# Stationary token tiles begin 64 bytes further in SBUF

## The reference

```python
# first block, per layer (w_in: 1024 x 10,432, cut into 12 parts)
h = rmsnorm(x, pre_norm_g[l])
(u, v, z_a, c_q, c_kv, k_rope, z_b, x_c, z_c, g_a, g_b, g_c) = split(h @ w_in[l])
y_a = gmlp_spatial(u, v, ...) * silu(z_a)
y_b = mla_attention(c_q, c_kv, k_rope, ...) * silu(z_b)
y_c = rg_lru(x_c, ...) * silu(z_c)
merged = (sigmoid(g_a) * (y_a @ w_proj_a[l]) + sigmoid(g_b) * (y_b @ w_proj_b[l])
          + sigmoid(g_c) * (y_c @ w_proj_c[l]))
x = x + rmsnorm(merged @ w_out[l], post_norm_g[l])

# second block, per layer: a pooling mixer (layer 0) or sparse attention (layer 1), then
x = x + conv_ffn(rmsnorm_2(x, norm_ffn[i]), ffn_up[i], ffn_conv[i], ffn_conv_b[i], ffn_down[i])
gate = sigmoid(rmsnorm_2(x, norm_ple[i]) @ ple_gate[i])
x = x + gate * (p[i] @ ple_proj[i])
```

## Time and profile before

| | |
|---|---|
| median of 3 runs | 1472.91 us (1466.99, 1472.91, 1478.4) |
| span of the profiled execution, first to last instruction | 1465.8 us |
| time of the profiled execution | 1465.8 us |
| TensorE busy | 1422.5 us, 97% |
| VectorE busy | 1051.1 us, 72% |
| ScalarE busy | 871.4 us, 59% |
| DMA | 240.98 MB, mean 164 GB/s |
| mean granted TensorE clock | 0.991 |

### The profile page before, as it was taken

The page is one execution under the profiler, slowest core; times in us unless marked ns, Lnnn a source line. Parts: engine busy times, 40 slices in busy tenths (PEclk is TensorE's granted clock), DMA queues, the critical chain, the costliest instruction groups (busy, mean ns, idle before and its releaser), DMA issues.

```text
span 1465.8 us, 23062 instructions
## 1 busy us (share of the span) xinstructions
PE 1422.5 (97%) x9283; PEld 1281.7 (87%) x9283; DVE 1051.1 (72%) x1601; ACT 871.4 (59%) x1522; POOL 85.3 (6%) x138
## 2 busy tenths in 40 slices
PE   8999999999999999999999989999989999999997
PEld 8988989888789989898878789998889878999886
DVE  7736669986676447699986778884776665888746
ACT  7465756564465656575545656664683553766546
POOL 9100000006000000000000000000000000000000
PEclk9999999999999999999999999999999999999999
DMA  8614476566556344665675537766545103666553
GB/s 256 189 50 151 124 228 195 180 193 190 193 145 186 80 123 144 188 189 185 188 223 199 158 116 220 214 202 191 158 145 145 45 1 104 208 191 197 185 180 115
DMA packets 189210, 240.98 MB, mean 164 GB/s; under 512 B 19086, under 2 KB 133954, under 8 KB 189104
## 3 DMA queue, kind: packets, MB, share of 16 engines
q1 hardware_dynamic: 183232, 228.66, 51.4%
q0 software_dynamic: 5776, 10.82, 2.3%
q10 hardware_dynamic: 96, 0.03, 0.0%
HBM read 238.42 MB, written 1.05 MB: 163 GB/s over the span
## 4 chain that ended last, share of the span: by engine, by line
PE 86%; ACT 5%; DVE 5%; DMA 2%; issue 1%; DVEq 0%; SPq 0%
PE bank L620 25%; PE bank L623 25%; PE bank L624 25%; PE bank L837 2%; PE bank L1222 1%; ACT w_hi L1327 1%; DVE w_lo L1883 1%; DMA raw<-in_mla_w_ukv 1%; ACT T L1824 1%; PE bank L1179 1%; PE bank L1136 1%; ACT S L1520 1%; PE bank L774 1%; PE bank L1208 1%; PE bank L900 0%
## 5 line engine op out<-in xcount | busy, mean ns | idle before, releaser
L1883 DVE TENSOR_TENSOR w_lo<-raw,w_hi 128x1024 fp32r<-128x1024 f32 (+2 forms) x452 | 518.6, 1170 | 207.9 <-ACT w_hi L1327 204.7
L1327 ACT CAST w_hi<-raw 128x1024 fp32r<-128x1024 f32 (+2 forms) x452 | 449.4, 1009 | 271.6 <-DMA raw<-in_w_in 114.3
L620 PE MATMUL bank<-h_hi,w_hi 128*128 128x256 f32 (+1 forms) x1640 | 457.4, 279 | 6.8 <-DVE h_lo L1919 3.9
L623 PE MATMUL bank<-h_lo,w_hi 128*128 128x256 f32 (+1 forms) x1640 | 454.8, 277 | 0.0
L624 PE MATMUL bank<-h_hi,w_lo 128*128 128x256 f32 (+1 forms) x1640 | 454.6, 277 | 0.0
L620 PEld LDWEIGHTS bank<-h_hi,w_hi 128*128 128x128 f32 (+1 forms) x1640 | 308.2, 188 | 10.0 <-issue 7.8
L623 PEld LDWEIGHTS bank<-h_lo,w_hi 128*128 128x128 f32 (+1 forms) x1640 | 308.2, 188 | 0.1
L624 PEld LDWEIGHTS bank<-h_hi,w_lo 128*128 128x128 f32 (+1 forms) x1640 | 308.1, 188 | 0.0
L620 PE MATMUL bank<-w_hi,h_hi 128*128 128x512 f32 (+1 forms) x464 | 178.8, 385 | 2.7 <-DVE h_lo L1919 1.7
L623 PE MATMUL bank<-w_lo,h_hi 128*128 128x512 f32 (+1 forms) x464 | 176.7, 381 | 0.0
L624 PE MATMUL bank<-w_hi,h_lo 128*128 128x512 f32 (+1 forms) x464 | 176.6, 381 | 0.0
(11 more groups left out here) (366 smaller groups left out, 2084.9 us busy)
## 6 DMA issues: line engine op xcount, KB each, us to landing
raw<-in_w_in SPq DMA_DIRECT2D x160, 512.0 KB, 3.8
raw<-in_ffn_up SPq DMA_DIRECT2D x88, 512.0 KB, 4.5
raw<-in_ffn_down SPq DMA_DIRECT2D x40, 512.0 KB, 4.4
raw<-in_w_proj_a SPq DMA_DIRECT2D x16, 512.0 KB, 3.6
raw<-in_w_proj_b SPq DMA_DIRECT2D x16, 512.0 KB, 3.5
raw<-in_w_proj_c SPq DMA_DIRECT2D x16, 512.0 KB, 3.6
raw<-in_w_out SPq DMA_DIRECT2D x16, 512.0 KB, 3.6
raw<-in_ple_gate SPq DMA_DIRECT2D x16, 512.0 KB, 4.6
```

Of the source, the lines that this page charges most:

```text
L620: first = pe.matmul(out_, lh, rh, start=start, stop=False)
L623: pe.matmul(out_, lh, rl, start=False, stop=False)
L1327: act.copy(weights(w_hi, slot, b, size), weights(raw, slot, b, size)).then_inc(sems["hi_done"], 1)
L1883: dve.tensor_tensor(weights(w_lo, slot, b, size), weights(raw, slot, b, size), weights(w_hi, slot, b, size).bitcast(F32), ALU.subtract).th ...
```

## The change

Tiles of tokens that are only ever stationary begin 64 bytes further in SBUF. For `y2`, `ya`, `yb`, `yc` and `p` this is done in the plans of `overlay`: a gap `steps(1)` of 64 bytes is put ahead of the pair, and gaps behind it are sized so that what follows keeps its place or moves as a whole. `h_hi` and `h_lo` become views of rooms that are 32 floats longer, and a second pair of views, `s_hi` and `s_lo`, begins 16 floats on. All uses in which `h` holds merged tokens, gated tokens (the input of the ple gate) or the attention's output go to `s`; the uses as the normed input `h` stay. `sg` and `rec` get other places, and the constant `causal1` is cut from 256 to 128 columns, which makes room and leaves the values in use as they were.

Begin of the operands of `three` in the built programs, in bytes modulo 128, and the count of its matmuls:

| columns | moving | stationary | count before | count after |
|---|---|---|---|---|
| 256 | 96 (tokens) | 32 (weights) | 5124 | 5124 |
| 256 | 96 (tokens) | 96 (weights) | 108 | 108 |
| 256 | 32 (weights) | 96 (tokens) | 144 | 144 |
| 512 | 96 (weights) | 96 (tokens) | 2496 | 816 |
| 512 | 96 (weights) | 32 (tokens) | 0 | 1680 |

Of the 108, 96 are those of `keys_values` and 12 belong to a product with 48 stationary columns. The order of instructions is the same on every engine before and after, and so are their waits and shapes, except that the constants' second load has 1476 columns instead of 1604.

```diff
-                  ("mask1", TOK), ("mask0", P), ("causal1", TOK), ("cmp0", 16), ...
+                  ("mask1", TOK), ("mask0", P), ("causal1", P), ("cmp0", 16), ...
-    put("causal1", np.where(k <= q + P, 0.0, -1e30))
+    put("causal1", np.where(k[:, :P] <= q, 0.0, -1e30))
...
+        def steps(n):
+            return (None, [P, SHIFT * n], F32)
...
-        h_hi = sb("h_hi", [P, KT, TOK], F32R)
-        h_lo = sb("h_lo", [P, KT, TOK], F32R)
+        h_room = [sb(name, [P, KT * TOK + 2 * SHIFT], F32R) for name in ("h_hi", "h_lo")]
+        h_hi, h_lo = (t[:, 0:KT * TOK].rearrange("p (k n) -> p k n", n=TOK) for t in h_room)
+        s_hi, s_lo = (t[:, SHIFT:SHIFT + KT * TOK].rearrange("p (k n) -> p k n", n=TOK) for t in h_room)
...
-             ("zc", [P, LT, TOK], F32)],
+             steps(2), ("zc", [P, LT, TOK], F32), ("rec", [P, 1, TOK], F32)],
...
-             ("yb_hi", [P, KT, TOK], F32R), ("yb_lo", [P, KT, TOK], F32R),
+             steps(1), ("yb_hi", [P, KT, TOK], F32R), ("yb_lo", [P, KT, TOK], F32R),
...
-             ("uz", [P, KT, TOK], F32), ("rec", [P, 1, TOK], F32), ("wsT", [P, GM_GROUPS, P], F32),
-             ("bs", [P, GM_GROUPS, P], F32), ("yc_hi", [P, LT, TOK], F32R), ("yc_lo", [P, LT, TOK], F32R)],
-            [kb(20), ("G", [P, KT, TOK], F32), ("ya_hi", [P, KT, TOK], F32R), ("ya_lo", [P, KT, TOK], F32R)],
+             ("uz", [P, KT, TOK], F32), steps(14), ("wsT", [P, GM_GROUPS, P], F32),
+             ("bs", [P, GM_GROUPS, P], F32), ("yc_hi", [P, LT, TOK], F32R), steps(2), ("yc_lo", [P, LT, TOK], F32R)],
+            [kb(20), ("G", [P, KT, TOK], F32), steps(1), ("ya_hi", [P, KT, TOK], F32R), ("ya_lo", [P, KT, TOK], F32R)],
...
-            [(None, [P, 9, TOK], F32), ("p_hi", [P, L * 2, TOK], F32R), ("p_lo", [P, L * 2, TOK], F32R), kb(3),
-             (None, [P, KT, TOK], F32),
-             ("y2_hi", [P, FT, TOK], F32R), ("y2_lo", [P, FT, TOK], F32R), ("ua", [P, 2, TOK], F32),
-             ("ug", [P, 2, TOK], F32), ("sg", [P, 2, TOK], F32)],
+            [steps(9 * 16 - 1), ("p_hi", [P, L * 2, TOK], F32R), ("p_lo", [P, L * 2, TOK], F32R),
+             steps(1), ("sg", [P, 2, TOK], F32), steps(16), (None, [P, KT, TOK], F32),
+             steps(1), ("y2_hi", [P, FT, TOK], F32R), ("y2_lo", [P, FT, TOK], F32R), ("ua", [P, 2, TOK], F32),
+             ("ug", [P, 2, TOK], F32)],
...
# TensorE: the out product of the first block (the same in gate_by_token and project2)
-            h = (h_hi, h_lo)
+            h, s = (h_hi, h_lo), (s_hi, s_lo)
-                tokens(1, 0, h, k0=4, start=False, ready="m_ready")
+                tokens(1, 0, s, k0=4, start=False, ready="m_ready")
-                tokens_in_turn([(0, 0), (1, 4)], 0, h)
+                tokens_in_turn([(0, 0), (1, 4)], 0, s)
...
# ScalarE and VectorE: the writes of these tokens (three pairs like this one)
-                        act.copy(h_hi[:, k:k + 2, :].rearrange("p a n -> p (a n)"), ps[b][:, :])\
+                        act.copy(s_hi[:, k:k + 2, :].rearrange("p a n -> p (a n)"), ps[b][:, :])\
...
-                        dve.tensor_tensor(h_lo[:, k:k + 2, :].rearrange("p a n -> p (a n)"), ps[b][:, :],
-                                          h_hi[:, k:k + 2, :].rearrange("p a n -> p (a n)").bitcast(F32), ALU.subtract)\
+                        dve.tensor_tensor(s_lo[:, k:k + 2, :].rearrange("p a n -> p (a n)"), ps[b][:, :],
+                                          s_hi[:, k:k + 2, :].rearrange("p a n -> p (a n)").bitcast(F32), ALU.subtract)\
```

More of the change, by code:

```diff
@@ L125 @@
 for _name, _n in (("ident", P), ("eps", 1), ("ones", P), ("swap1", P), ("swap2", P), ("cos1", TOK), ("sin1", TOK),
-                  ("mask1", TOK), ("mask0", P), ("causal1", TOK), ("cmp0", 16), ("cmp1", 16), ("cmo0", 16), ("cmo1", 16),
+                  ("mask1", TOK), ("mask0", P), ("causal1", P), ("cmp0", 16), ("cmp1", 16), ("cmo0", 16), ("cmo1", 16),
                   ("freq", 4)):
@@ L964, in _ @@
                 w.go("m_ready", KT)
-                tokens(0, 0, h, stop=False, ready="m_ready", only=(0,))
+                tokens(0, 0, s, stop=False, ready="m_ready", only=(0,))
                 turn_merged(1)
@@ L970, in _ @@
                         transposes([p_in[:, n, t, f * P:(f + 1) * P] for f in range(2) for t in range(TT)])
-                tokens(0, 0, h, stop=False, ready="m_ready", only=(1,))
-                tokens(1, 0, h, k0=4, start=False, ready="m_ready")
+                tokens(0, 0, s, stop=False, ready="m_ready", only=(1,))
+                tokens(1, 0, s, k0=4, start=False, ready="m_ready")
                 w.go("S", 2), w.go("J", 2)
-                tokens_in_turn([(0, 0), (1, 4)], 0, h)
+                tokens_in_turn([(0, 0), (1, 4)], 0, s)
                 w.go("S", 2), w.go("J", 2)
@@ L1059, in piece @@
                         tok, cols = slice(t * P, (t + 1) * P), slice((k - ka) * 512, (k - ka + 1) * 512)
-                        three(ps[banks[t]][:, :], h_hi[:, k, tok], h_lo[:, k, tok], weights(w_hi, slot, b)[:, cols],
+                        three(ps[banks[t]][:, :], s_hi[:, k, tok], s_lo[:, k, tok], weights(w_hi, slot, b)[:, cols],
                               weights(w_lo, slot, b)[:, cols], k == 0, False, k == ka and (half == 0) == (t == 0))
@@ L1068, in gate_by_token @@
                 w.go("ht_ready", 2 * KT)
-                tokens(1, 0, h, k0=4, start=False, ready="ht_ready")
+                tokens(1, 0, s, k0=4, start=False, ready="ht_ready")
                 w.go("S", 2)
-                tokens_in_turn([(0, 0), (1, 4)], 2, h)
+                tokens_in_turn([(0, 0), (1, 4)], 2, s)
                 w.go("S", 2), w.go("J", 4)
@@ L1251, in project2 @@
                             cols = slice(n * 512, (n + 1) * 512)
-                            mm = three(ps[bank][:, :], h_hi[:, k, t * P:(t + 1) * P], h_lo[:, k, t * P:(t + 1) * P],
+                            mm = three(ps[bank][:, :], s_hi[:, k, t * P:(t + 1) * P], s_lo[:, k, t * P:(t + 1) * P],
                                        weights(w_hi, slot, b)[:, cols], weights(w_lo, slot, b)[:, cols], k == 0, k == KT - 1, begins)
@@ L1404, in split_token @@
                     at = (k // 2) * P
-                    act.activation(h_hi[:, k, t * P:(t + 1) * P], ps[b][:, at:at + P], ACT.Identity, scale=gain(k))\
+                    act.activation(s_hi[:, k, t * P:(t + 1) * P], ps[b][:, at:at + P], ACT.Identity, scale=gain(k))\
                         .then_inc(sems["ht_hi"], w.given("ht_hi"))
@@ L1755, in _ @@
             act.copy(ident_r[:, :], c["ident"])
-            act.copy(causal_r[:, :], c["causal1"][:, P:TOK]).then_inc(sems["masks_r"], 1)
+            act.copy(causal_r[:, :], c["causal1"]).then_inc(sems["masks_r"], 1)
             def split_h2(tiles):
@@ L1835, in high_o @@
                 act.wait_ge(full[b], w.turn(*ring))
-                act.copy(h_hi[:, 2 * g:2 * g + 2, :].rearrange("p a n -> p (a n)"), ps[b][:, :])\
+                act.copy(s_hi[:, 2 * g:2 * g + 2, :].rearrange("p a n -> p (a n)"), ps[b][:, :])\
                     .then_inc(sems["o_hi_done"], w.given("o_hi_done"))
@@ L1933, in low_token @@
                     dve.wait_ge(sems["ht_hi"], w.taken("ht_hi"))
-                    dve.scalar_tensor_tensor(h_lo[:, k, tok], ps[b][:, at:at + P], gain(k), h_hi[:, k, tok].bitcast(F32),
+                    dve.scalar_tensor_tensor(s_lo[:, k, tok], ps[b][:, at:at + P], gain(k), s_hi[:, k, tok].bitcast(F32),
                                              ALU.mult, ALU.subtract).then_inc(sems["ht_ready"], w.given("ht_ready"))
@@ L2692, in low_o @@
                 dve.wait_ge(sems["o_hi_done"], w.taken("o_hi_done"))
-                dve.tensor_tensor(flat(h_lo[:, 2 * g:2 * g + 2, :]), ps[b][:, :],
-                                  flat(h_hi[:, 2 * g:2 * g + 2, :]).bitcast(F32), ALU.subtract)\
+                dve.tensor_tensor(flat(s_lo[:, 2 * g:2 * g + 2, :]), ps[b][:, :],
+                                  flat(s_hi[:, 2 * g:2 * g + 2, :]).bitcast(F32), ALU.subtract)\
                     .then_inc(free[b], 1)
```

## The result

The changed kernel is slower: 1497.53 us (median of 6 runs, 1493.43 to 1503.26) against 1474.74 us before (6 runs), ratio 1.0157, 95% interval 1.0135 to 1.0179. The profiled span went from 1465.8 to 1493.7 us, 27.9 us more. The forecast was 1463.4, with 1474.0 as the upper end of its range.

What follows compares the result with a forecast made beforehand. TensorE was taken to bound the kernel: span 1465.8 - 10.1 (1680 matmuls x 6 ns) + 0.6 (VectorE in `ya`) = 1456.3 us; the difference of 9.5 carried to the median 1472.91 gave 1463.4 us, range 1452 to 1474.

Steps and rivals of the forecast that it cites:

- TensorE bounds the kernel, time per matmul is time of the kernel.: Whole kernel: TensorE is busy 1422.5 of 1465.8 us, its longest waits total 6.3, 6.0 and 5.6 us.
- Equal places cost 5.8 ns at 256 columns.: `keys_values` (moving and stationary both at 96) against `features` (96/32): 119.1 - 113.3 = 5.8 ns per matmul.
- The load is 128 columns in both cases, so the collisions of one load should cost about the same.: 512-column matmuls: the 5.8 ns read at 256 columns was carried over, taken as 6 ns saved each.
- The term of 1680 x 6 = 10.1 us less: TensorE's 1680 512-column matmuls on shifted tokens: 6 ns saved on each, 10.1 us in all.
- The rival of no change: 512-column matmuls: the load's delay is hidden, the stream's loss has another cause; 0 saved, 1472.9 us; chance 0.19.
- the 17.5 ns at 512 columns: Down stage: 230.8 ns per matmul against 213.3 for its columns; the remainder the change was said to reach for.
- Features must stay at 113.3.: Sign for `features`, whose stationary tile isn't moved: its 256-column matmuls keep 113.3 ns in the profile after.
- the other edits: Writes of shifted tiles, moved `sg` and `rec`, smaller `causal1`: 0, or a few tenths of a us at the beginning.
- if these move too, the place isn't the cause: Sign: `features` leaving 113.3 ns or the ga, gb, gc stages leaving 231 would rule out the stationary tile's place.
- The slower rival: 512-column matmuls: the stream meets the load on more steps, 5.8 ns each, 9.7 us more, 1482.6 us; chance 0.06.
- The Trainium skill's rule: TensorE: two independent read ports, so loading weights takes no read bandwidth from the running matmul; the sum would be 0.
- VectorE's share in `ya`: Stage `ya`: VectorE, busy 21.75 of 22.20 us, limits the saving; 0.3 us off per layer, 0.6 in all.

Runs made afterwards that it cites:

- mov32: Changed kernel with h's pair as before, and weight pieces of 2- and 4-k-tile slots begun 64 bytes further; first half of `keys_values` 119.4 to 114.0 ns, single run.
- split_plain: Kernel before, with 512-column matmuls on y2, ya, yb, yc and p (but first and last of a group) cut into two of 256; y2 118.3 ns, single run.
- split_shift: shift256 with 512-column matmuls on shifted tokens (but first and last of a group) cut into two of 256; ratio 1.0033, y2 117.6 ns.
- half_sta: Kernel before, with 64 of 128 stationary columns used in the down product's first column half; 230.8 ns per matmul there.
- shift256: Changed kernel with h_hi's room 64 floats longer than the tile instead of 32, so h_lo lies 8192 + 256 bytes behind; 1475.3 us, ratio 0.9994.
- both128: Kernel before, with h_hi and h_lo moved together by 128 bytes, their distance kept at 8192; `features` 114.1 ns, single run.
- align64: Kernel before, with x and all behind it 32 bytes further, so operands begin at 0 or 64 modulo 128; ratio 1.0018.
- wlo128: Kernel before, with w_lo moved by 128 bytes against w_hi, so the weight pair lies a multiple of 256 bytes apart; ratio 1.0027.
- combo: shift256 plus a 32-float gap ahead of the landing buffers, so the moving weight pair is also a multiple of 256 bytes apart; ratio 1.0019.

## Why the prediction was wrong, point by point

- *TensorE bounds the kernel, time per matmul is time of the kernel.* Right: 27.3 us more TensorE time made 27.9 us more span.
- *Equal places cost 5.8 ns at 256 columns.* Right as a reading, and mov32 shows it by undoing it. But it holds for stationary weights; with tokens stationary, split_plain and split_shift put it at 0.7 ns.
- *"The load is 128 columns in both cases, so the collisions of one load should cost about the same."* This is the step that took the gain away: a cost seen at 256 columns was carried to 512. There a load half as long leaves the pace as it was (half_sta, 230.8), and every place tried, the weights' distance and the alternation move it by 2 ns at most. The term of 1680 x 6 = 10.1 us less measured 1.4 us more in the changed kernel, and nothing in its time with the distance mended (shift256, ratio 0.9994). The rival of no change had that time; its mechanism, a load that is hidden at 512 columns, fits half_sta, but isn't shown beyond it.
- The prediction had the hint in its own numbers: `features` with a 64-column load ran at 113.3 ns like the full one. It took this to mean that the load no longer disturbs the stream at 96/32, and didn't ask whether the 17.5 ns at 512 columns had ever been the load's.
- *"Features must stay at 113.3."* This is the step that made the sign wrong. The diff says `KT * TOK + 2 * SHIFT`, and the front part's table of places modulo 128 shows nothing of it, since 8320 is 0 modulo 128. The longer rooms stand in no term of the sum, not even among "the other edits": they were put at nothing without a reason. They cost 6.2 ns on each of 4704 matmuls, 29 us. The sign set for it, "if these move too, the place isn't the cause", came: `features` moved, and the cause was the distance of the moving pair.
- *The slower rival*, with a chance of 0.06, had the right side but another mechanism and stage: collisions in the 512-column products, at 1482.6 us. That the time rose bears it out in nothing.
- *The Trainium skill's rule* ("TensorE: Matmul & The Clock Gate", Part 2, Step-by-step), that a load takes no read bandwidth from the running matmul, agrees with the 512-column products (half_sta: 0 ns for half a load). It doesn't explain mov32's 5 to 6 ns from the place of what is loaded, at 256 columns.
- *VectorE's share in `ya`* never came to be tested, since nothing was saved there.

## What to carry to other kernels

When a tile's room is made longer, ask what else moves: the distance of two tiles that are read in turn is a quantity of its own, and a table of places must be taken at more than one modulus. Here a hi/lo pair that moves through TensorE at 256 columns (h) ran at 113.6 to 114.6 ns on average when it was a multiple of 256 bytes apart, and at 118 to 120 when 64 or 128 bytes more. Look at stretches too and not only at the mean of a group: single stretches at 119 showed that another quantity counts. Before a gain at one size is carried to another, test on the chip what it hangs on: a run with half the load would have shown that the 17.5 ns per 512-column matmul don't hang on its length.

## What was not expected of the hardware

- Two moving tiles read in turn cost 4 to 7 ns on each 256-column float32r matmul when they lie 64 or 128 bytes apart modulo 256 (118.0 and 119.8 against 113.6 ns on h; 120.2 against 113.4 on c, 119.9 against 114.0 on h2). It isn't paid at the seam between them, it is gone when one isn't read, and a stationary tile of 64 columns doesn't spare it (117.4 against 113.3).
- At a granted clock of 0.50 the same products start 213.3 ns apart whatever the distance or the place. All that is lost is lost at the full clock, where 256 columns would be 106.7 ns.
- At 256 columns stretches run at one of two paces, some 113.3 or some 118 to 119 ns, also where the pair is a multiple of 256 bytes apart. Moving the pair against the weights by 128 bytes changed which stretches are slow (both128).
- The place of stationary weights against moving tokens, 64 bytes apart modulo 128 or equal, is worth 5 to 6 ns at 256 columns (mov32). The place against the 64-byte line changed nothing but one stretch on h2 (align64).
- 512-column float32r matmuls with stationary tokens took 230 to 233 ns in all groups of the table in every trace, some 17 more than 512 columns at one per cycle of 2.4 GHz (213.3), whatever was changed. What takes these 17 ns stays open, as does the rule that joins the distances of the moving and the stationary pair at 256 columns (wlo128 and combo raised h2 to 116.7 and 117.8 while one group of tokens fell to 113.4).
